# A blocked triangular inverse in a recurrent scan: the last level on its 64x64 corner, in half the rows of the array

## The reference, cut to what matters

```python
def rwkv7_scan(r, w, k, v, kk, a, S0, reverse):
    ...
    def step(S, inp):
        w_t, k_t, v_t, kk_t, b_t = inp[:5]
        sa = jnp.einsum('bhvk,bhk->bhv', S, kk_t)
        S = (S * w_t[:, :, None, :] - sa[..., None] * b_t[:, :, None, :]
             + v_t[..., None] * k_t[:, :, None, :])
        o = jnp.einsum('bhvk,bhk->bhv', S, inp[5]) if with_out else None
        return S, o

    S, o = lax.scan(step, S0, xs, reverse=reverse)
```

## Time and profile before

| | us |
|---|---|
| median of 3 runs | 4714.99 (4713.99 to 4716.72) |
| the profiled execution, its own time | 4711.24 |
| its span | 4709.4 |
| TensorE busy | 4538.0 (96%) |
| VectorE busy | 2683.1 (57%) |
| ScalarE busy | 1728.4 (37%) |
| GpSimd busy | 428.9 (9%) |
| VectorE, the masks G (L1556), 560 instructions | 376.8 |
| TensorE, F of all levels (L1336), 1600 matmuls | 272.2 |

### The profile page before, as it was taken

One profiled execution on the slowest core, in us unless ns is written; L12 is line 12 of the kernel. 1 busy time (PEld: TensorE's weight loads), 2 busy tenths in 40 slices (PEclk: granted clock), 3 DMA queues, 4 the chain that ended last, 5 costly groups with the idle time before them and its releaser, 6 DMA issues. The chain is left out here.

```text
span 4709.4 us, 66517 instructions
## 1 busy us (share of the span) xinstructions
PE 4538.0 (96%) x27608; PEld 3680.5 (78%) x27608; DVE 2683.1 (57%) x3962; ACT 1728.4 (37%) x2924; POOL 428.9 (9%) x347
## 2 busy tenths in 40 slices
PE   8999999999999999999999799899998789999999
PEld 5888877778998888888888544688777567888887
DVE  3245545555636766676667676546453755555543
ACT  3233444345524444444444343311343742111111
POOL 0000000000012322332232000000010000000000
PEclk9999999999999999999999899999999989999999
DMA  5344433344430110111022244333120021212222
GB/s 207 109 141 143 144 138 137 141 150 157 138 109 19 40 58 28 63 40 58 28 82 62 85 134 139 107 126 126 55 78 15 23 112 56 75 67 76 95 94 94
DMA packets 155978, 441.79 MB, mean 94 GB/s; under 512 B 17168, under 2 KB 47120, under 8 KB 140448
## 3 DMA queue, kind: packets, MB, share of 16 engines
q1 hardware_dynamic: 140624, 383.98, 23.3%
q0 software_dynamic: 9296, 32.58, 1.9%
q10 hardware_dynamic: 5760, 20.97, 1.2%
HBM read 294.86 MB, written 141.56 MB: 93 GB/s over the span
## 5 line engine op out<-in xcount | busy, mean ns | idle before, releaser
L202 PE MATMUL pr_ps<-uhl,w_split 128*128 128x512 f32 (+1 forms) x1520 | 585.8, 385 | 3.1 <-DVE w_split L145 2.2
L206 PE MATMUL pr_ps<-uhl,w_split 128*128 128x512 f32 (+1 forms) x1520 | 570.8, 376 | 0.0
L205 PE MATMUL pr_ps<-uhl,w_split 128*128 128x512 f32 (+1 forms) x1520 | 570.4, 375 | 0.0
L1556 DVE TENSOR_TENSOR b_G<-b_ps,cst 128x512 fp32r<-128x512 f32 x560 | 376.8, 686 | 80.7 <-PE b_ps L1336 79.2
L138 ACT ACTIVATE w_split<-share 128x2048 fp32r<-128x2048 f32 x64 | 122.6, 1916 | 701.0 <-DVE ou_vc L3301 271.1
L202 PEld LDWEIGHTS pr_ps<-uhl,w_split 128*128 128x128 f32 x1520 | 286.5, 188 | 81.5 <-issue 29.2
L205 PEld LDWEIGHTS pr_ps<-uhl,w_split 128*128 128x128 f32 x1520 | 286.7, 189 | 55.9 <-issue 5.8
L206 PEld LDWEIGHTS pr_ps<-uhl,w_split 128*128 128x128 f32 x1520 | 286.4, 188 | 52.5
L1336 PE MATMUL b_ps<-b_G,b_EY 128*128 128x128 f32 x1600 | 272.2, 282 | 20.0 <-DVE b_G L1556 19.4
L1124 POOL TENSOR_SCALAR b_Mr<-b_tri 128x512 fp32r<-128x512 f32 x80 | 117.7, 1488 | 1890.0 <-DVE b_tri L1540 1890.0
L202 PE MATMUL ou_ps<-ou_a,w_split 128*128 128x512 f32 x704 | 277.3, 394 | 7.7 <-DVE ou_a L2156 7.7
(11 more groups left out here) (498 smaller groups left out, 10035.4 us busy)
## 6 DMA issues: line engine op xcount, KB each, us to landing
w_ring<-in_w_in SPq DMA_DIRECT2D x41, 1024.0 KB, 5.2
proj<-pr_stage SPq DMA_DIRECT2D x160, 256.0 KB, 2.0
share<-in_w_up SPq DMA_DIRECT2D x24, 1024.0 KB, 4.8
ar<-share SPq DMA_DIRECT2D x32, 512.0 KB, 2.8
b_AR<-ar SPq DMA_DIRECT2D x64, 256.0 KB, 2.9
pr_raw<-proj SPq DMA_DIRECT2D x48, 256.5 KB, 3.5
ada<-in_ada_w SPq DMA_DIRECT2D x24, 512.0 KB, 5.7
ff<-ou_vc ACTq DMA_DIRECT2D x24, 512.0 KB, 2.6
```

Source lines behind the costliest of these rows:

```text
L202: mm = nc.tensor.matmul(dst, a[0], b[0], start=start, stop=False)
L205: nc.tensor.matmul(dst, a[0], b[1], start=False, stop=False)
L206: return nc.tensor.matmul(dst, a[1], b[0], start=False, stop=stop)
L1556: L[x]["dve"].done(V.tensor_tensor(Gs[x][m % 2][:], heads(x, 0 if m else 1), rep(K(f"lev{m}"), 4), ALU.mult), f"{n}.G{m}")
```

## The change

Level 6 has one off-diagonal block per system: 64x64, rows of one half and columns of the other. The change computes only that block. F5 becomes eight matmuls that contract over 64 rows (`rest[x]`) with 64 columns, alternating between x = 0 (rows 0 to 63 of the array) and x = 1 (rows 64 to 127). G6 on VectorE becomes a multiplication by -1 of the 64x64 corners (64 partitions, 256 numbers each) in place of the mask over 128x512. Y6 becomes eight such matmuls over the other half (`edge[x]`), and ScalarE copies back the 64x64 corners only. On TensorE both Y5 now stand ahead of F5, both transposes of A and B behind both Y6. The names of the steps in `level_names` follow.

```diff
@@ -1009,6 +1009,9 @@
         heads = lambda x, b: ps[:, 4 * x + b].rearrange("p (q f) -> p q f", q=4)
         by_head = lambda t: t.rearrange("p (t h c) -> p h t c", t=2, h=2)
         spare = lambda h: bank(h, 3)
+        edge = [slice(64, P), slice(0, 64)]
+        rest = [slice(0, 64), slice(64, P)]
+        corners = lambda x, b: bank(x, b)[:, 0:256].rearrange("p (q f) -> p q f", q=4)
         both = lambda x: ps[:, 4 * x + 1:4 * x + 3].rearrange("p b (q a f) -> p (b q) a f", q=2, a=2)
 
         last = LEVELS - 1
@@ -1021,7 +1024,7 @@
         high_on_dve = lambda x: x == 1
 
         def level_names(n, x):
-            return {"pe": ["F0", "E0"] + sum(([f"F{m}", f"EY{m}"] for m in range(1, 5)), []) + ["F5", "Y5", "Y6"],
+            return {"pe": ["F0", "E0"] + sum(([f"F{m}", f"EY{m}"] for m in range(1, 5)), []) + ["Y5", "F5", "Y6"],
                     "act": ["E0"] + sum(([f"low{m}"] + ([] if high_on_dve(x) else [f"high{m}"]) for m in range(1, 5)), []) + ["Y5", "Y6"],
                     "dve": ["G0", "G1"] + sum(([f"G{m}"] + ([f"high{m - 1}"] if high_on_dve(x) and m < LEVELS - 1 else []) for m in range(2, LEVELS)), [])}
 
@@ -1190,9 +1193,13 @@
                     if not high_on_dve(x):
                         L[x]["act"].done(A(EY[x][:, 2:4], both(x)[:, 2:4], ACT.Copy), f"{n}.high{m}")
 
-                def y_out(i, n, x, m):
-                    L[x]["pe"].wait(act, i, f"{n}.Y{m}")
-                    L[x]["act"].done(A(Y[x], heads(x, 2), ACT.Copy), f"{n}.Y{m}")
+                def y_out(i, n, x):
+                    L[x]["pe"].wait(act, i, f"{n}.Y5")
+                    L[x]["act"].done(A(Y[x], heads(x, 2), ACT.Copy), f"{n}.Y5")
+
+                def corner_out(i, n, x):
+                    L[x]["pe"].wait(act, i, f"{n}.Y6")
+                    L[x]["act"].done(A(Y[x][rest[x], :, edge[x]], corners(x, 2)[rest[x]], ACT.Copy), f"{n}.Y6")
 
                 def solved(i, n, x):
                     B[x]["pe"].wait(act, i, f"{n}.C0")
@@ -1350,26 +1357,43 @@
                         mm = mmul(both(x)[:, q], Gs[x][m % 2][:, q], EY[x][:, q], start=True, stop=True)
                     L[x]["pe"].done(mm, f"{n}.EY{m}")
 
-                def y_next(i, n, x, m):
-                    L[x]["dve"].wait(pe, i, f"{n}.G{m}")
-                    if m == 6:
+                def y_five(i, n, x):
+                    L[x]["dve"].wait(pe, i, f"{n}.G5")
+                    L[x]["act"].wait(pe, i, f"{n}.low4")
+                    high(x).wait(pe, i, f"{n}.high4")
+                    L[x]["pe"].done(quad(bank(x, 2), Gs[x][1], Y[x]), f"{n}.Y5")
+
+                def corner_f(i, n):
+                    for q in range(4):
+                        for x in range(2):
+                            mm = mmul(corners(x, 0)[:, q], E[x][rest[x], q], Gs[x][1][rest[x], q, rest[x]], start=True, stop=True)
+                            if q == 3:
+                                L[x]["pe"].done(mm, f"{n}.F5")
+
+                def corner_y(i, n):
+                    for x in range(2):
+                        L[x]["dve"].wait(pe, i, f"{n}.G6")
                         L[x]["act"].wait(pe, i, f"{n}.Y5")
-                    L[x]["pe"].done(quad(bank(x, 2), Gs[x][m % 2], Y[x]), f"{n}.Y{m}")
+                    for q in range(4):
+                        for x in range(2):
+                            mm = mmul(corners(x, 2)[:, q], Gs[x][0][edge[x], q], Y[x][edge[x], q, edge[x]], start=True, stop=True)
+                            if q == 3:
+                                L[x]["pe"].done(mm, f"{n}.Y6")
 
                 def levels(i, n):
-                    for m in range(1, 6):
+                    for m in range(1, 5):
                         for x in range(2):
                             f(i, n, x, m)
-                            if m < 5:
-                                ey(i, n, x, m)
-                            else:
-                                y_next(i, n, x, m)
+                            ey(i, n, x, m)
                         if m == 1 and i and n == 0:
                             mean(i - 1)
                         if m == 1 and i and n == 1:
...
+                    for x in range(2):
+                        y_five(i, n, x)
+                    corner_f(i, n)
 
                 def solve(i, n, x):
                     i_, n_ = before(i, n)
@@ -1464,9 +1488,9 @@
                     if nxt:
                         turn_kv(*nxt, 0)
                         turn_kv(*nxt, 1)
-                    for x in range(2):
-                        y_next(i, n, x, last)
-                        if nxt:
+                    corner_y(i, n)
+                    if nxt:
+                        for x in range(2):
                             turn_ab(*nxt, x)
                     solve(i, n, 0)
                     solve(i, n, 1)
@@ -1553,6 +1577,9 @@
                         F[x]["pe"].wait(dve, i, f"{n}.XT")
                     else:
                         L[x]["pe"].wait(dve, i, f"{n}.F{m - 1}")
+                    if m == last:
+                        L[x]["dve"].done(V.tensor_scalar(Gs[x][0][edge[x], :, rest[x]], corners(x, 0)[edge[x]], -1.0, None, ALU.mult), f"{n}.G{m}")
+                        return
                     L[x]["dve"].done(V.tensor_tensor(Gs[x][m % 2][:], heads(x, 0 if m else 1), rep(K(f"lev{m}"), 4), ALU.mult), f"{n}.G{m}")
 
                 def high_out(i, n, x, m):
```

More of the change, by code:

```diff
@@ L1218, in _ @@
                     for x in range(2):
-                        y_out(i, n, x, 5)
+                        y_out(i, n, x)
                     if nxt:
@@ L1223, in _ @@
                     for x in range(2):
-                        y_out(i, n, x, last)
+                        corner_out(i, n, x)
                     for x in range(2):
```

## The result

The changed kernel is **slower**: 4736.73 us median (4730.85 to 4740.18, 4 runs) against 4715.85 (4713.99 to 4718.93, 4 runs); the ratio is 1.0045, its 95% interval 1.0032 to 1.0057. That is 20.9 us more. The forecast was 4713.3, with a range from 4698 to 4729.

The account below looks back on a forecast made before the run. TensorE's queue in the scan was taken as the bound; C0 0.1 us later a unit, less 0.14 to 0.16 given back downstream, made -1.7 us over 39 units: 4714.99 to 4713.3 us, range 4698 to 4729.

Parts of the forecast that it names:

- What bounds: In the scan, TensorE's queue is the bound or close to it: busy 1236.78 of 1262 us.
- The half-row block: F5 and Y6 corners: eight loads take 0.33 us, not 0.78; way in 0.26, out 0.26; switches cost 0.15 to 0.2.
- No gain from removing F5 of direction 0, Y5 no earlier: That F5 stood where TensorE waited, so removal gives nothing; direction 1's Y5 starts at 1880.90, no earlier than its F5 did.
- G6 is there by 1883.0, and the corners come at 1883.1: Before the Y6 corners: two VectorE copies finish while TensorE transposes K and V, with 0.1 to 0.2 us to spare.
- the sum: TensorE's path in one unit, Y5 of direction 1 to C0: 3.57 us, putting C0 at 1884.47, 0.1 us later.
- G6 comes late: Rival: Y6 corners wait if G6's two copies take over 0.95 us; s = 0.48, +13 us, 4728; chance 0.10.
- s: Shift of C0's start in one unit against the kernel before: forecast 0.1 us later.
- what is given back: Downstream of C0, shorter waits for ScalarE's copies return 0.14 us a unit, 0.16 where the next has n = 0.
- 39 s - 5.6: Whole time change in us over 39 units, 32(s - 0.14) + 7(s - 0.16): -1.7 us with s = 0.1.
- the clock: TensorE's granted clock, read as 0.99 in the scan; the forecast had no term or rival for a change in it.
- slower: Sign of the result: slower by over 0.2%, from late G6, halves that don't overlap and a tail; chance 0.18.

Follow-up runs that it names:

- experiment 5: Kernel before, its order kept, with half-row corner matmuls, four of one direction at a time, and short copies: 4764.3 us, ratio 1.0102.
- experiment 1: Kernel before with only the changed TensorE order; matmuls, masks and copies full size: 4734.8 us, ratio 1.0042.
- experiment 3: Changed kernel with corner matmuls over all 128 rows, 64 columns, so no half-row mode in them: 4746.2 us, ratio 1.0071 to the kernel before.
- experiment 2: Changed kernel with G6 of direction 1 on ScalarE, direction 0's still on VectorE: 4717.7 us, ratio 1.0009 to the kernel before.
- experiment 6: Changed kernel with VectorE's affine step of the pair before moved behind G6: 4722.0 us, ratio 1.0010 to the kernel before.
- experiment 8: Changed kernel run again, unaltered: 4735.0 us, ratio 1.0045 to the kernel before.
- experiment 7: Kernel before with VectorE's affine step moved behind G6: 4705.7 us, ratio 0.9984.
- experiment 9: Old order, full-row corners, short copies, VectorE tail steps behind G6: three moved 4701.7 us, all four 4689.7; changed order, G6 split over VectorE and ScalarE, three moved: 4700.5.

## Why the prediction was wrong

- *What bounds:* right. TensorE's queue and its hand-overs set every unit.
- *The half-row block:* right to 0.03 us. 0.33 us from the first to the last load of F5 and 0.36 of Y6, 0.24 out of either (0.26 worked out), switches dear; experiment 5 confirms that only two halves together gain.
- *No gain from removing F5 of direction 0, Y5 no earlier:* right, and experiment 1 shows that this is what the order costs: what stood in a wait went onto the path.
- **The step that failed: "G6 is there by 1883.0, and the corners come at 1883.1. The transposes of K and V hide it, with 0.1 to 0.2 us to spare."** On that clock G6 was there at 1883.10 (1889.71 in the trace), and the corners came at 1883.32. Three terms were short. The corners' end and VectorE's start behind it came 0.07 later. Two VectorE copies of 64x256 took 0.88 us and not 0.82, 0.422 us each and one strictly behind the other, where two full masks overlap (1.28 us for two of 0.69). And the hand-over from G6's end to the first load took 0.22 us, in 37 of 40 units, which the sum put at nothing. This last is the largest: TensorE itself was ready 0.30 behind the last load, at 1883.13, so without it G6 would have been just in time. Why it takes 0.22, where Y5 in a unit with n = 2 starts 0.11 behind the copy that it waited for, stays open; it isn't the switch to half rows, for it is 0.22 with full rows too (experiment 3). The wait delays the corners by 0.19 us a unit, and experiment 2, where G6 is ready in time, takes 0.20 off. It is the rival "G6 comes late", at half its price, though the two copies stayed under the 0.95 us from which that rival was to decide.
- *The rest of s:* the Y5 quads and the way into the corners 0.06, the Y6 block 0.03, the transposes of A and B 0.04, less 0.05 on the ways out of the two blocks and in the transposes of K and V: s = 0.10 + 0.19 + 0.08 = about 0.36. The rule for what is given back was near: s - 0.14 forecast, 0.36 to 0.17 or 0.13 measured, 0.19 to 0.23. With the measured s, 39 s - 5.6 is 8.4 us, against 7.1 in 36 units.
- *Left out:* the units with n = 2. The prediction took one unit for all and didn't look at what else VectorE does in others. There the high copy is late, and a whole quad waits for it where before only the third matmul did: 0.29 us more, six times 0.29, 1.7 us.
- **The other step that failed, a term that the sum put at nothing:** the clock. The traces of the changed kernel have two and three units of 36 at 4.6 us more, with the granted clock at 0.50 for 10 us of each; 9 to 14 us, more than everything else. No rival spoke of it, though the earlier trace rows put the clock at 0.99 in the stage. Experiments 2 and 6 had no long unit in 36 and were 19 and 15 us faster than the change, of which their shorter units explain 7 and 2.5. What starts a drop stays open: experiments 3 and 5 have them in units to n = 0 and n = 3 too, equal units of one trace differ in it (experiment 8), and experiment 2's trace has none though its n = 2 units are still 0.23 us longer than before. No run filled TensorE's waits with other matmuls.
- *The sign and the range:* "slower" had 0.18, and of the cases behind it one was at work, at half its price. By the regular part alone, 7 us, the kernel would have come out near 4722, inside the range though of the wrong sign; the long units put it outside.

## What to carry to other kernels

Work that an engine does while it waits is free; an edit that shrinks it but moves it behind the wait pays for what is left of it. When a block of half-row matmuls replaces full ones, count its two switches and give both halves loads in turn: eight alternating loads take 0.33 us in place of 0.78, four of one half the same 0.33 as in full. Alternating two results also makes both of them ready only at the end, so ask who waits for the first. Add the hand-over between engines to every wait that is said to be just hidden. Where a wait ends last, try its producer split over two engines, which gave 0.20 us a unit here, and put an engine's side work where it idles: that was worth more here (experiments 7 and 9) than the whole change was meant to be.

## What the runs showed of the hardware

- Two VectorE copies of 64x256 from PSUM to float32r, 422 ns each, took 0.88 us, with no overlap; two of 128x512 of 0.69 us took 1.28 us. ScalarE's two of 64x256 took 0.78 us, 379 ns each.
- A gap put down to "issue" can be a wait: 0.35 us ahead of the Y6 corners in 39 units fell to 0.17 once G6 was made sooner.
- From the end of G6 on VectorE to the first weight load of the Y6 corners passed 0.22 us, with half rows and with full rows; from the end of the high copy to Y5's first load 0.11 us.
- The granted clock of TensorE fell to 0.50 for about 10 us in some of several equal units and not in others, 4.6 us each, in both traces of the changed kernel; TensorE was busy for 5.8 of the 7 us ahead in units that dropped and in units that didn't.
